# Second conditioning pair computed in the first stage instead of the gates, with the loads and norms of x reordered

## The reference

```python
mod = jax.nn.silu(c) @ w_ada + b_ada
sh1, sc1, ga1, sh2, sc2, ga2 = jnp.split(mod[:, None, :], 6, axis=-1)
h = rms_norm(x, g_pre1) * (1.0 + sc1) + sh1
u = h @ w_in
...
merged = jax.nn.sigmoid(za) * (y_ret @ w_br_ret) + jax.nn.sigmoid(zb) * (y_hg @ w_br_hg)
x = x + ga1 * rms_norm(merged @ w_out, g_post1)
h2 = rms_norm(x, g_pre2) * (1.0 + sc2) + sh2
x = x + ga2 * rms_norm(expert_choice_ffn(h2, w_router, w_gate, w_up, w_down), g_post2)
```

## Time and profile before

| engine | busy us | share |
|---|---|---|
| PE matmul | 2665.3 | 93% |
| DVE | 1786.0 | 63% |
| ACT | 1335.4 | 47% |
| POOL | 301.6 | 11% |

### The profile page before, as it was taken

One profiled execution on the slowest core, in us unless ns is written; L12 is line 12 of the kernel. 1 busy time (PEld: TensorE's weight loads), 2 busy tenths in 40 slices (PEclk: granted clock), 3 DMA queues, 4 the chain that ended last, 5 costly groups with the idle time before them and its releaser, 6 DMA issues. The chain is left out here.

```text
span 2854.7 us, 48423 instructions
## 1 busy us (share of the span) xinstructions
PE 2665.3 (93%) x20566; PEld 2132.8 (75%) x20566; DVE 1786.0 (63%) x2147; ACT 1335.4 (47%) x1410; POOL 301.6 (11%) x246
## 2 busy tenths in 40 slices
PE   5999999999999988983999999999999999999993
PEld 3788888889877877862777777777777777777772
DVE  4675757767400054547777777776777777777775
ACT  5544435354211121441555555555555555555552
POOL 2010000101000011211011101110111101110110
PEclk9999999999999999995999999999999999999996
DMA  7111011011343265236788788788888888887886
GB/s 283 33 31 44 24 35 55 23 52 31 115 158 126 72 209 166 97 105 242 276 286 298 286 300 289 276 295 291 294 289 296 295 289 284 282 300 286 284 290 230
DMA packets 285775, 564.97 MB, mean 198 GB/s; under 512 B 24680, under 2 KB 91080, under 8 KB 285304
## 3 DMA queue, kind: packets, MB, share of 16 engines
q1 hardware_dynamic: 274536, 540.79, 53.2%
q0 software_dynamic: 7680, 20.98, 3.2%
q10 hardware_dynamic: 3344, 0.11, 0.1%
HBM read 514.52 MB, written 47.28 MB: 197 GB/s over the span
## 5 line engine op out<-in xcount | busy, mean ns | idle before, releaser
L2291 DVE TENSOR_TENSOR we_low<-ring,we_high 128x2048 fp32r<-128x2048 f32 x384 | 878.1, 2291 | 366.5 <-ACT we_high L2240 366.5
L2240 ACT ACTIVATE we_high<-ring 128x2048 fp32r<-128x2048 f32 x384 | 737.4, 1922 | 438.9 <-PE ps_ey L2212 279.7
L1297 PE MATMUL ps_a<-h_high,w_high 128*128 128x512 f32 (+1 forms) x696 | 252.7, 363 | 7.7 <-ACT pair L817 4.8
L1298 PE MATMUL ps_a<-h_low,w_high 128*128 128x512 f32 (+1 forms) x696 | 247.6, 356 | 0.0
L1299 PE MATMUL ps_a<-h_high,w_low 128*128 128x512 f32 (+1 forms) x696 | 247.4, 356 | 0.0
L2179 PE MATMUL ps_ep<-ring,xp 128*32 128x256 f32 x4096 | 234.3, 381 | 0.0
L2210 PE MATMUL ps_ey<-we_high,hidT_high 128*128 128x512 f32 x512 | 206.6, 403 | 0.0
L2154 PE MATMUL ps_eg<-we_high,xs_high 128*128 128x512 f32 x512 | 206.2, 403 | 0.3 <-DVE xs_low L2315 0.3
L2179 PEld LDWEIGHTS ps_ep<-ring,xp 128*32 128x32 f32 x4096 | 126.6, 110 | 99.5 <-issue 22.5
L2156 PE MATMUL ps_eu<-we_high,xs_high 128*128 128x512 f32 x512 | 200.3, 391 | 0.0
L2157 PE MATMUL ps_eu<-we_low,xs_high 128*128 128x512 f32 x512 | 200.2, 391 | 0.0
(11 more groups left out here) (308 smaller groups left out, 4976.3 us busy)
## 6 DMA issues: line engine op xcount, KB each, us to landing
ring<-in_w_gate SPq DMA_DIRECT2D x256, 512.0 KB, 9.4
ring<-in_w_up SPq DMA_DIRECT2D x256, 512.0 KB, 10.5
ring<-in_w_down SPq DMA_DIRECT2D x256, 512.0 KB, 4.4
w_raw<-in_w_in SPq DMA_DIRECT2D x52, 512.0 KB, 3.8
w_ring<-in_w_ada SPq DMA_DIRECT2D x12, 1024.0 KB, 11.1
sig_dram<-sig SPq DMA_DIRECT2D x15, 640.0 KB, 7.1
w_ada_z<-in_w_ada SPq DMA_DIRECT2D x16, 512.0 KB, 6.9
sig_g<-sig_dram SPq DMA_DIRECT2D x16, 512.0 KB, 3.8
```

Of the source, the lines that this page charges most:

```text
L1297: pe.matmul(out, w_high, x_high, start=start, stop=False)
L1298: pe.matmul(out, w_high, x_low, start=False, stop=False)
L2240: act.activation(w_high[:, s % SPLIT], t.ring[:, s % RAW], ACT.Copy).then_inc(s_high, 1)
L2291: dve.tensor_tensor(w_low[:, s % SPLIT], t.ring[:, s % RAW], w_high[:, s % SPLIT], ALU.subtract).then_inc(s_low, 1)
```

## The change

The first stage computes all five parts 0 to 4 (20 pieces instead of 12), `columns` and `scale_shift` run there a second time at its end, and the gates have nothing of it left, nor the clearing of the heads' semaphores by SP. The order of the loads is new, three pairs of x are normed ahead of the loop over tiles and two inside it, and the parts 2 to 4 share one bank of PSUM, so that the first piece of parts 3 and 4 waits until DVE has taken the part before.

```diff
-        PARTS = 3
+        PARTS = 5
...
-        ps_mod, ps_col = [ps_mod0, ps_x[2]], ps_x[3]
+        ps_mod, ps_col = [ps_mod0, ps_x[2], ps_mod0, ps_mod0, ps_mod0], ps_x[3]
...
 # SP
+            load_w(0)
+            load_w(1)
             load_x(0)
-            load_w(0)
+            load_w(2)
+            load_w(3)
             load_x(1)
-            load_w(1)
+            load_w(4)
             load_x(2)
-            load_w(2)
+            load_w(5)
+            load_head(0)
+            load_w(6)
+            load_w(7)
             load_x(3)
-            load_w(3)
+            load_w(8)
             load_x(4)
-            load_head(0)
-            for j in range(4, NJ):
+            for j in range(9, 4 * PER):
                 load_w(j)
...
 # PE
-                    pe.wait_ge(s_modsb, v - 1)
+                    pe.wait_ge(s_modsb, max(v, 2))
...
-                if 2 <= tl < 2 + PER:
-                    mod_rows(COLS1 + tl - 2)
-                if tl in (6, 7):
-                    project(0, KC // 2 * (tl - 6), KC // 2 * (tl - 5))
-            project(1, 0, KC)
+                if tl >= 3:
+                    mod_rows(COLS1 + tl - 3)
+                if tl in (6, 8):
+                    project(0, KC // 4 * (tl - 6), KC // 4 * (tl - 4))
+            mod_rows(4 * PER - 1)
+            project(1, 0, KC // 2)
+            mod_rows(4 * PER)
+            project(1, KC // 2, KC)
+            mod_rows(4 * PER + 1)
             project(2, 0, KC)
+            mod_rows(4 * PER + 2)
+            mod_rows(4 * PER + 3)
+            pe.wait_ge(s_modsb, PARTS)
...
+            columns((3, 4))
 # ACT
-                act.dma_start(pre_cols[:], t.g_pre1[0].rearrange("(c p) -> p c", p=P)).then_inc(s_small, 16)
+                for n, v in enumerate((t.g_pre1, t.g_pre2)):
+                    act.dma_start(pre_cols[:, n], v[0].rearrange("(c p) -> p c", p=P)).then_inc(s_small, 16)
...
+                if tl in (1, 3):
+                    squares(3 + tl // 2)
+                if tl in (3, 5):
+                    root(3 + tl // 4)
 # DVE
-                if tl == 8:
+                if tl == 2:
+                    variance(3)
+                if tl == 4:
+                    norm(3)
+                    variance(4)
+                if tl == 6:
+                    norm(4)
+                if tl == 7:
                     rows(2)
                     gate_row(2)
...
+            rows(3)
             low(NT - 1)
+            rows(4)
+            scale_shift(1, t.scale2[:], t.shift2[:])
 # gates, PE
-                    if 3 <= k < 3 + KC and b != 1:
-                        ada(2 * (k - 3) + b // 2)
-                    if k == KC + 4 and b == 0:
-                        columns()
```

More of the change, by code:

```diff
@@ L218, in mod_rows, with columns @@
                 if i == 0 and v >= 2:
-                    pe.wait_ge(s_modsb, v - 1)
-                mm = ada_rows(pe, ps_mod[v % 2], c_pad, w_ring[:, j % NW], i)
+                    pe.wait_ge(s_modsb, max(v, 2))
+                mm = ada_rows(pe, ps_mod[v], c_pad, w_ring[:, j % NW], i)
                 mm.then_inc(s_mod, 1)
-            def columns():
-                for v in range(2):
+            def columns(parts):
+                for k, v in enumerate(parts):
                     for h in range(2):
-                        o = (2 * v + h) * P
+                        o = (2 * k + h) * P
                         mm = pe.transpose(ps_col[:, o:o + P], mod[:, v, h * P:(h + 1) * P], t.ident[:])
@@ L246, in _ @@
             pe.wait_ge(s_modsb, 2)
-            columns()
+            columns((0, 1))
             def project(b, c0, c1):
@@ L300, in _ @@
             act.activation(lb_low[:], lb_diff[:], ACT.Sigmoid).then_inc(s_lb, 1)
-            for i in range(NX):
+            for i in range(3):
                 squares(i)
@@ L304, in _ @@
                     root(i - 1)
-            root(NX - 1)
+            root(2)
             act.wait_ge(s_first, 16)
@@ L355, in gate_row, with variance @@
                 dve.tensor_tensor(post[:], mod[:, v], post[:], ALU.mult).then_inc(s_rows, 1)
-            def norm(i):
+            def variance(i):
                 v = ssum[:, 2 * i:2 * i + 2]
@@ L376, in _ @@
             head_columns()
-            for i in range(NX):
+            for i in range(3):
+                variance(i)
                 norm(i)
@@ L1324, in phase_branch_gates @@
         s_w = [sem(f"w{i}") for i in range(3)]
[L1325 to L1333, removed]
         block = ctx.enter_context(nc.Block())
@@ L1356, in _ @@
                 sp.dma_start(t.yT[:, m], t.yT_dram[m].rearrange("h p n -> p h n")).then_inc(t.s_branch, 16)
[L1357 to L1365, removed]
             for k in range(1, NG):
@@ L1374, in _ @@
                 sp.wait_ge(s_store[i], 16 * len([k for k in range(1, NG) if k % 3 == i]))
-        @block.gpsimd
-        def _(pool):
-            pool.memset(c_pad[:], 0.0)
-            pool.memset(bias[:], 0.0)
-            pool.drain()
-            pool.sem_inc(s_zero, 1)
         @block.tensor
         def _(pe):
-            def ada(j):
-                pe.wait_ge(s_wa[j % 2], 16 * (j // 2 + 1))
-                if j == KC:
-                    pe.wait_ge(s_rows, 1)
-                k = j % KC
-                for g in range(4):
-                    mm = pe.matmul(ps_mod[32 * g:32 * g + 32, 0:QW], c_pad[:, k], w_a[:, j % 2, g * QW:(g + 1) * QW],
-                                   start=(k == 0), stop=(k == KC - 1), tile_position=(0, 32 * g))
-                mm.then_inc(s_ada, 1)
-            def columns():
-                pe.wait_ge(s_rows, 2)
-                for v in range(2):
-                    for h in range(2):
-                        o = (2 * v + h) * P
-                        mm = pe.transpose(ps_col[:, o:o + P], mod[:, v, h * P:(h + 1) * P], t.ident[:])
-                mm.then_inc(s_col, 1)
             for k in range(1, NG):
@@ L1414, in _ @@
                     mm.then_inc(s_mm, 1)
-                    if k == 3 and b == 0:
-                        pe.wait_ge(s_pad, 1)
-                    if 3 <= k < 3 + KC and b != 1:
-                        ada(2 * (k - 3) + b // 2)
-                    if k == KC + 4 and b == 0:
-                        columns()
         @block.scalar
@@ L1430, in _ @@
             high(2)
-            act.wait_ge(s_zero, 1)
-            act.activation(c_pad[:, :, 0:2], t.c_silu[:], ACT.Copy).then_inc(s_pad, 1)
             for k in range(1, NG):
```

56 lines of the change are left out of this document (17 added, 39 removed).

## The result

| kernel | median us | range | executions |
|---|---|---|---|
| before | 2853.53 | 2850.98 to 2857.42 | 16 |
| changed | 2859.4 | 2857.26 to 2860.36 | 16 |

The ratio is 1.0019, 95% interval [1.0011, 1.0026]: slower by 5.9 us in the medians, 3.1 to 7.4 by the interval. The forecast was +5.4. The changed kernel's profiled execution took 2859.65 us, its span is 2857.8. Tiles are counted from 0, so the seventh tile is tile 6.

The account below looks back on a forecast made before the run. PE bounds the gates; SP's queue bounds the first stage up to the columns, ACT and DVE set the pace behind them. First stage +23.0 and gates -17.6 give +5.4, a median of 2859.6 us, range 2850 to 2868.

Parts of the forecast that it names:

- The gates: Groups 1 to 15 of the gates: PE loses ada calls, transposes, piece waits and slower clock, -17.6 us.
- Columns: First stage up to the columns: they come at 44.0 us instead of 45.38, -1.4 us.
- The rule of one for one: ACT and SP queues, first stage: packets move one for one, so 1024 added gather packets are worth 10.4 us.
- Columns to the seventh tile: From columns to the seventh tile's turn: four squares and a norm inside the loop delay it, +7.7 us.
- From there to the end: Seventh tile's turn to first stage's end: more pieces, 3.9 us standing and a new tail, 33.1 us, +11.7.
- The clock: First stage, behind PE's two stands: half clock costs 0 to 5 us together, taken as 3.0.
- the shared port: First stage: POOL's norms beside DVE's loop make three operations lose 0 to 2.3 us, taken as 1.2.
- the tail: End of the first stage: copy 0.4, transposes 0.6, shift and scale 0.7, hops 0.6, together 2.3 us.
- The stage: The whole first stage: -1.4 + 7.7 + 11.7 + 5.0, so +23.0 us.
- Rival 1: First stage: `c_pad` stays at 12, small vectors come late, columns at 51; time 2866.6 us, chance 0.19.
- Rival 2: First stage: gather costs next to nothing, `c_pad` at 12, columns at 41, clock kept; 2852.4 us, chance 0.20.
- Rival 3: First stage: PE's stands fill themselves, the stage is PE's work alone, +2.8 us; time 2839.5 us, chance 0.11.

Follow-up runs that it names:

- gather only: The kernel before plus one gather of g_pre2 on ACT behind g_pre1, its data read by nobody; 2857.57 us, one profiled execution.
- three edits: The changed kernel with g_pre2's gather behind `c_pad`, part 2 copied before tile 7's evacuation, and squares and norms earlier; 2847.85 us, ratio to before 0.9977.
- tail hidden: The kernel of three edits with the last pieces put before block 2 and the second columns in its middle; 2846.41 us, ratio to before 0.9977.
- packed: Changed kernel: gather later, squares earlier, one more piece behind tile 3, part 2 copied at tile 6, pieces 16-19 within block 1, columns mid block 2; 2850.9 us.
- gather late: The changed kernel with ACT issuing the gather of g_pre2 behind `c_pad`, on its own semaphore; 2856.54 us, one profiled execution.
- squares early: The changed kernel with pair 3's squares ahead of the loop, pair 4's at tile 1, norms at tiles 1 and 4; 2853.36 us, one profiled execution.
- order only: The changed kernel's load order and in-loop norms, but 12 pieces, no g_pre2 gather, parts 3 and 4 left in the gates; 2860.71 us, one profiled execution.
- Copy first: The changed kernel with DVE copying part 2 in front of its evacuation of tile 7; 2851.23 us, one profiled execution.

## Why the forecast came out where it did

**The gates (-17.6)**: right in the traces, 17.62, and 17.1 to 17.6 with all three profiles of before. In the timed executions it may be less. The traces sum to +19.6 - 17.6 = +2.0, and the profiled executions differ by as much (2858.24 and 2859.65 against a median of 2856.98), while the timed ones differ by 5.9. A saving of 13.5, which holds where no piece is late ("gather only"), would give +6.1. The same sum made for the other timed kernels asks for a saving of 15.4 (three edits), 15.2 (tail hidden) and 16.9 (packed). So the term that I read as one number is a range of 13.5 to 19. That it is nearer its low end without the profiler is only argued: no trace shows such an execution. The rival that the difference lies in the first stage or the heads is open too, since they moved by 1.8 and 2.8 us over profiles.

**Columns (-1.4)**: -3.4. The step that missed is the one that had the columns at 44.0, on a `c_pad` at 22 and a queue of SP dry from 21.3 to 24.0. `c_pad` was at 18.89, since 490 of the 1024 added packets went through in the first 6 us (2218 packets against 1727 of before), when SP's queue moves small elements too. SP's queue only ran at half its rate for 2 us, and "gather late" shows that even 6.7 us of `c_pad` are worth about 1 us here. I charged it 3. The rule of one for one was right, its place was not: in the old order the small packets cost what the vectors behind them wait for, 6.6 us, and in the new one, where the vectors are in time, 1.4 to 1.9 us at the columns (41.94 and 42.44 against 40.59).

**Columns to the seventh tile (+7.7)**: +7.4 (20.1 for 20.5), with the stand of 4.59 put down to the norm. Shown by "squares early" and, on its own, by "order only".

**From there to the end (+11.7, and +5.0 left out)**: +15.7, 1.0 less than the 16.7. The wait for the copy was 3.79 for 3.9. The clock cost 4.1 and not 3.0 (3.2 in the second profile, at these five calls); the shared port 0 for 1.2 (in-loop norms 0.75, `h_low` 1.23, once 1.34); the tail 1.6 (97.42 to 99.05) for 2.3. "Copy first" shows that wait and clock belong together, 5.45.

**The stage**: +19.6 for +23.0. **The sum**: +5.4 forecast, +5.9 [3.1, 7.4] measured, and +2.0 by the profiles. That the sum is this close is luck: the stage's error of 3.4 and the gates' uncertain saving lie on opposite sides. The stated range of 18 us also took in rivals 1 and 2, so meeting it says little. What the runs do bear out is the mechanism (both stands, their releasers and the half clock behind them); two sizes were off, the columns and the gates' saving.

**The rivals.** Rival 1 (late vectors) is what the old order does with the gather (columns at 51.95, forecast 51), not the new one; its `c_pad` at 12 came in neither. Rival 2's columns at 41 nearly came true (41.94), its `c_pad` at 12 and its clock did not. Rival 3 (the stands fill themselves) was wrong for this order of the lists, but three moved lines bring much of it: 2847.85, and 2846.41 with the tail hidden.

## What to carry to other kernels

Work moved into a stage that "has room" must be placed against each engine's list. Here the room was real, and two list places, a norm behind squares and a copy behind a low half, gave back some 10 us of it; moving them, with the gather, moved the mark by 10.3. A stand of PE costs its length and then the half clock behind it, so a stand of 3.8 us was worth 5.4. A stand of 2.5 us in the kernel before cost its length alone in two profiles and 1.8 us more in the third, so near that length the price is no single number. Before calling a term a saving, profile the old kernel more than once, and a neighbour with the same code in that stage: three profiles of before agreed on the gates within 0.5 us, and two neighbours lay 4.2 below and 1.6 above the first.

## What the runs showed that was not expected

- ACT's issues are held while its queue has much outstanding: with the gather two issues took 5.06 and 5.21 us, without it one of 4.49 ("gather late") or 4.21. Each time the hold ended when some 1230 to 1270 of its small packets were still outstanding (issued less moved, without the held transfer itself). That this number is what holds the issue is read from these four holds; no run varied it.
- The kernel before takes 2853.5 us in timed executions and 2857.0 in three profiled ones; the changed kernel 2859.4 and 2858.9. What makes the profiled executions of before longer is open; timed ones as long do occur (2857.42, 2857.76 and 2858.11), but they are 3 of over 50.
- The heads, which no edit touches, took 696.4 to 699.2 us over the profiles (first `w_high` to the gates' first sigmoid of group 1).
- DVE's `w_low` took 1.93 us beside POOL's norm and 1.23 here, beside two others of POOL's norms (35.40 to 41.50): running beside it is not enough to slow it.
